# The SSD's products inside a chunk, each issued as two products on the two column halves of the array

## What is computed

```python
cs = jnp.cumsum(da, axis=-1)
causal = jnp.tril(jnp.ones((Q, Q), dtype=bool))
seg = cs[..., :, None] - cs[..., None, :]
lmat = jnp.where(causal, jnp.exp(jnp.where(causal, seg, 0.0)), 0.0)
cb = jnp.einsum('bclgn,bcsgn->bcgls', cm, bm)
y_diag = jnp.einsum('bcgls,bcgels,bcsgep->bclgep', cb, lmat, xdt)
...
y = y_diag + y_off + xs * d_skip.astype(f32).reshape(G, E, 1)
```

## Time and profile before

| | us |
|---|---|
| median of 3 runs | 2791.63 |
| lowest and highest run | 2790.51, 2798.21 |
| the profiled execution, its own time | 2796.33 |
| its span, first to last instruction | 2795.1 |
| TensorE busy in the span | 2762.6 (99%) |
| VectorE busy | 1732.2 (62%) |
| ScalarE busy | 1347.7 (48%) |

### The profile page before, as it was taken

The page is one execution under the profiler, slowest core; times in us unless marked ns, Lnnn a source line. Parts: engine busy times, 40 slices in busy tenths (PEclk is TensorE's granted clock), DMA queues, the critical chain, the costliest instruction groups (busy, mean ns, idle before and its releaser), DMA issues.

```text
span 2795.1 us, 40891 instructions
## 1 busy us (share of the span) xinstructions
PE 2762.6 (99%) x17151; PEld 2361.5 (84%) x17151; DVE 1732.2 (62%) x2043; ACT 1347.7 (48%) x1741; POOL 42.4 (2%) x71
## 2 busy tenths in 40 slices
PE   8999989999999999999999999999999999999998
PEld 7888887888888888888888888888888888888887
DVE  6787667654655655555555566556766656665675
ACT  6745434544554444434444545554554444443444
POOL 2000000000000000000000100000000000000001
PEclk9999999999999999999999999999999999999999
DMA  7565327566555656666666555555556555565553
GB/s 235 168 196 188 98 68 234 171 197 195 156 175 181 188 190 195 191 190 191 196 185 193 181 189 187 166 171 176 175 173 195 189 191 193 181 196 196 190 187 136
DMA packets 395317, 506.69 MB, mean 181 GB/s; under 512 B 11441, under 2 KB 287422, under 8 KB 394366
## 3 DMA queue, kind: packets, MB, share of 16 engines
q1 hardware_dynamic: 380925, 488.26, 54.3%
q10 hardware_dynamic: 14208, 15.81, 1.8%
HBM read 501.87 MB, written 2.17 MB: 180 GB/s over the span
## 4 chain that ended last, share of the span: by engine, by line
PE 96%; DVE 2%; ACT 1%; DMA 1%; issue 1%; ACTq 0%; SPq 0%; DVEq 0%
PE PS L697 38%; PE PS L702 34%; PE PS L706 17%; PE PS L952 3%; PE PS L745 1%; PE PS L1182 0%; PE PS L1162 0%; DVE wlo L2184 0%; PE PS L728 0%; PE PS L874 0%; PE PS L1239 0%; DMA slab<-in_x 0%; PE PS L890 0%; ACT whi L1495 0%; PE PS L855 0%
## 5 line engine op out<-in xcount | busy, mean ns | idle before, releaser
L2184 DVE TENSOR_TENSOR wlo<-raw,whi 128x1024 fp32r<-128x1024 f32 x922 | 1128.4, 1229 | 787.6 <-ACT whi L1495 783.6
L1495 ACT ACTIVATE whi<-raw 128x1024 fp32r<-128x1024 f32 x922 | 970.6, 1057 | 931.4 <-PE PS L706 454.8
L702 PE MATMUL PS<-XX,whi 128*128 128x512 f32 (+1 forms) x3856 | 1215.8, 396 | 0.2
L706 PEld LDWEIGHTS PS<-XX,wlo 128*128 128x128 f32 (+1 forms) x3856 | 724.4, 188 | 171.2
L706 PE MATMUL PS<-XX,wlo 128*128 128x256 f32 (+1 forms) x3856 | 759.6, 278 | 0.0
L697 PE MATMUL PS<-whi,act 128*128 128x512 f32 x2208 | 593.1, 390 | 0.0
L702 PEld LDWEIGHTS PS<-XX,whi 128*128 128x128 f32 (+1 forms) x3856 | 588.9, 189 | 3.1 <-issue 1.6
L697 PEld LDWEIGHTS PS<-whi,act 128*128 128x128 f32 x2208 | 411.8, 188 | 83.9
L697 PE MATMUL PS<-wlo,act 128*128 128x512 f32 x1104 | 339.9, 389 | 0.0
L697 PE MATMUL PS<-whi,XX 128*128 128x512 f32 x1024 | 280.7, 396 | 7.4 <-DVE wlo L2184 3.1
L697 PEld LDWEIGHTS PS<-wlo,act 128*128 128x128 f32 x1104 | 207.2, 188 | 43.4
(11 more groups left out here) (417 smaller groups left out, 1428.6 us busy)
## 6 DMA issues: line engine op xcount, KB each, us to landing
raw<-in_ffn_w SPq DMA_DIRECT2D x128, 1024.0 KB, 5.5
raw<-in_w_in SPq DMA_DIRECT2D x103, 1024.0 KB, 5.0
raw<-in_w_ffn_gate SPq DMA_DIRECT2D x44, 1024.0 KB, 4.9
raw<-in_w_ffn_up SPq DMA_DIRECT2D x44, 1024.0 KB, 4.9
raw<-in_w_ffn_down SPq DMA_DIRECT2D x44, 1024.0 KB, 5.2
raw<-in_w_out SPq DMA_DIRECT2D x32, 1024.0 KB, 5.2
raw<-in_xattn_wk SPq DMA_DIRECT2D x16, 1024.0 KB, 5.5
raw<-in_xattn_wv SPq DMA_DIRECT2D x16, 1024.0 KB, 5.0
```

Source lines behind the costliest of these rows:

```text
L702: T.matmul(ps[0:wd, f, :], whi[:, o:o + wd], b.x[:, kk, :], start=first, stop=False, skip_group_check=True)
L706: mm = T.matmul(ps[0:wd, f, 0:SEQ], wlo[:, o:o + wd], b.x[:, kk, 0:SEQ], start=False, stop=last, skip_group_check=True)
L1495: S.activation(k.whi[:, h % 4, 0:b.size], k.raw[:, t % 4, u * b.size:(u + 1) * b.size], ACT.Copy).then_inc(k.w_hi, 1)
L2184: V.tensor_tensor(k.wlo[:, h % 4, 0:b.size], k.raw[:, h // 2 % 4, u * b.size:(u + 1) * b.size], k.whi[:, h % 4, 0:b.size].bitcast(F32), AL ...
```

## The change

Each product of line 855 becomes two. The first takes tokens s 0 to 63 as rows and tokens l 0 to 63 as columns (64 rows by 64 columns, at the array's first row and first column) and writes partitions 0 to 63 of the bank. The second takes all 128 tokens s as rows and tokens l 64 to 127 as columns (128 rows by 64 columns, in the second column half), and writes partitions 64 to 127. The quarter of `Ldec` that is left out is zero by the mask. Both move the same 64 channels. Nothing else is changed; the semaphore's increment stays on the last product of a block.

```diff
         for e in range(4):
             h = 8 * g + 4 * q + e
-            mm = T.matmul(PS[:, ssd_bank(n), (4 * q + e) * 64:(4 * q + e) * 64 + 64], k.Ldec[n % 3][:, e, :],
-                          k.xdt[:, c, h * 64:h * 64 + 64], start=(q == 0 and e == 0), stop=True,
-                          skip_group_check=True)
+            L, out, own = k.Ldec[n % 3], slice((4 * q + e) * 64, (4 * q + e) * 64 + 64), slice(h * 64, h * 64 + 64)
+            T.matmul(PS[0:64, ssd_bank(n), out], L[0:64, e, 0:64], k.xdt[0:64, c, own], start=(q == 0 and e == 0),
+                     stop=True, skip_group_check=True)
+            mm = T.matmul(PS[64:P, ssd_bank(n), out], L[:, e, 64:P], k.xdt[:, c, own], start=(q == 0 and e == 0),
+                          stop=True, skip_group_check=True)
         mm.then_inc(sd.pe, 1)
```

## The result

| | us |
|---|---|
| before, median of 12 runs | 2790.78 (2789.32 to 2798.21) |
| after, median of 12 runs | 2796.57 (2796.03 to 2800.59) |
| ratio after/before | 1.0016, 95% interval 1.0009 to 1.0023 |
| the profiled execution after, its own time | 2796.29 |
| its span | 2795.1 |

The change makes the kernel slower by 0.16%: 4.5 us by the ratio (2.5 to 6.4), 5.8 us by the medians. It was forecast at +5.9 us, and as no change within 0.3%. How near to 5.9 the true difference lies, the interval leaves open.

What follows compares the result with a forecast made beforehand. TensorE, busy 99% of the span, was taken to bound the kernel. Holds add 8.2 us, less 1.1 hidden behind block 2 and 1.2 in instruction gaps: +5.9, so 2797.5 us; range 2788 to 2801.

Steps and rivals of the forecast that it cites:

- A change of rows alone holds TensorE: Inside line 855's blocks: each of seven inner changes between 64 and 128 rows costs a hold of 0.145 us.
- The side-by-side rival: In line 855's blocks: column halves run together without holds, a block takes 0.66 us, total 2789.2 us; chance 0.16.
- The price: Line 855's blocks: a half product takes 0.255 us, eight take 2.04 us instead of 1.04.
- The sum on TensorE: All eight blocks: 3.4 us for blocks 3, 4, 5, 7 plus 4.8 for the others, +8.2 us before cover.
- The term for block 2: Behind block 2 TensorE waits 0.94 us for line 2609, hiding all but 0.1 of the block's 1.2 us: -1.1.
- The instruction gaps: Between 352 and 361 us TensorE runs out of instructions, 2.5 us in all; slower blocks close half, -1.2 us.
- The three gaps I had looked at: TensorE's three idle times between 352 and 361 us, 2.5 us in all, expected to be about half after.
- 3.8 us for a batch: Time TensorE needs for 256 instructions of 64x64 work at 0.029 us a step; transfers come one per 4.2 us.
- The 4.6 at the lower end of the range: Whole kernel: 8.2 - 1.1 - 2.5, the added time if all 2.5 us of gaps hide it.
- what I called no change: Whole kernel: a difference within 0.3% (8.4 us), hardly measurable; chance of this outcome 0.82.
- the working with nothing covered: From 330 to 361 us: gaps stay and 128 more instructions add up to 1.9 us: 8.2 - 1.1 + 1.9 = +9.0.
- The slower rival: From 330 to 361 us: holds with nothing covering them, gaps stay, +9.0 to +10.1 us, 2801 us; chance 0.15.

Runs made afterwards that it cites:

- Experiment 1: The change with both half products on all 128 rows, so one shape; 2789.25 us against 2791.17 of before, ratio 0.9989 (0.9980 to 0.9998).
- the second trace: The kernel before, unchanged, profiled once more; stretch between two fixed VectorE instructions 119.3 us against 120.9 in the first trace, span 2788.4 us.
- experiment 4: The change in blocks 3, 4 and 5 alone, the other blocks as before; one trace, stretch 123.1 us against 120.9 of before.
- experiment 5: The change in block 2 alone, the other blocks as before; one trace, stretch 121.1 us against 120.9 of before.
- experiment 6: The kernel before with 64 more transposes (128 TensorE instructions) at the start of TensorE's program; stretch 120.2 us against 120.9, total 2796.0 us.
- experiment 3: The change with both products 64 rows by 64 columns, leaving out part of the computation; one trace, stretch 118.9 us against 120.9 of before.

## Why the prediction was right

- **A change of rows alone holds TensorE.** The step on which all rested, and the one that no row of before showed for 64 and 128 rows in the same columns. Experiment 1 takes the change of shape away, with as many instructions, and the block falls from 2.05 to 0.62 us. The side-by-side rival had the right speed for the two halves, and the wrong condition: they do run at once, 0.01 us apart, if their shapes agree.
- **The price.** 0.255 us for a half product, measured 0.256; a block 2.04, measured 2.05; after line 697 the first load 0.31 us behind the last matmul, measured 0.32. The drain that the Trainium skill names ("TensorEngine Tiling (Array Packing)", Tiling Modes) is this 0.15 us. It is the 64 elements' stream and, by an estimate, about 0.1 us behind it: the holds of 0.21 us after 256 elements and 0.31 after 512 leave 0.11 that does not grow with them.
- **The sum on TensorE.** 8.2 less 1.1 behind block 2 was 7.1; the rest column of the table gives 121.8 - 113.9 = 7.9 (8.1 against the second trace). The 8.2 was right: matched matmul by matmul, a block behind line 697 or 851 adds 1.21 or 1.22 us, and blocks 3, 4 and 5 alone (experiment 4) 0.86, 0.87 and 0.83. The term for block 2 was right in its mechanism (experiment 5 shows VectorE not later). It was 1.2 against the first trace of before and 0.7 against the second, whose wait for line 2609 is 0.49 us instead of 0.94. What the sum lacked is a wait that a gap had covered. The rows are of before, of the change and of experiment 6:

```profile
400.65 0.35 PE L952 MATMUL PS<-over_x,slab 64*64 64x64 f32 x9 [1.39 <-issue]
...
405.50 0.44 PE L867 MATMUL PS<-ident,slab 128*128 128x128 f32 x2 [1.01 <-DVE slab L2513]
...
406.05 0.44 PE L865 MATMUL PS<-ident,slab 128*128 128x128 f32 x2 [1.01 <-DVE slab L2513]
```

  In before a batch ends (number 9153) just ahead of the products of line 865. While TensorE waits for its instructions, VectorE ends what these need (line 2511 there, at 400.34 us), and TensorE finds it done. With the count moved by 128, in the change as in experiment 6, no such gap stands there, and TensorE waits 1.01 us for VectorE; 0.28 us of a later wait goes in return, and 0.8 stays. With it the sum is 8.2 - 1.2 + 0.8 = 7.8 against the first trace (measured 7.9) and 8.2 - 0.7 + 0.8 = 8.3 against the second (8.1). Experiment 6, which adds no work here, has a rest 1.2 us above before's; 0.8 of it is this wait.
- **The instruction gaps.** I took 1.2 us of cover. The table has 7.0 - 4.4 = 2.6 against the first trace of before and 1.2 against the second. The three gaps I had looked at closed but for 0.14 us (I had said half); others opened, 0.47, 1.25 and 0.28 us. That the gaps belong to the instructions' count is shown by experiment 6, and that slower work closes the next ones by experiment 4. Their size differs by 1.4 us between two executions of one kernel, so no sum can be closer here. One term was misread: 3.8 us for a batch came from loads that step by 0.029 us, but in the products behind 352.73 they step by 0.015, and the batch that begins there has all begun within 2.0 us, 1.75 us ahead of the next.
- **The total.** +5.9 forecast; +5.8 by the medians, +4.5 by the ratio (2.5 to 6.4). Against the first trace of before the last two points erred by 0.8 up and 1.4 down, against the second by 1.0 up and nothing; the stretch was longer by 5.3 and 6.9. So it is partly luck that the medians met the forecast so closely. The 4.6 at the lower end of the range is a sum; 8.4 is the bound of what I called no change, where the working with nothing covered gave 9.0.
- **The slower rival** needed the gaps to stay. They shrank.
- **What would beat it.** I had bounded a gain at 4.2 us and given the halves none. With equal shapes the kernel gains 1.9 us by the medians and 3.1 by the ratio (0.6 to 5.6; experiment 1). Its blocks are shorter by 2.6 us (0.22 us behind lines 697 and 851, 0.42 behind line 954, four each). In the stretch 2.1 of it is left against the first trace of before, whose gaps are as large, and 0.5 against the second, whose gaps are 1.3 us less; the wait of 1.01 us for VectorE is there too.

Not tried: three products of 64 rows by 64 columns for each head, which would need no hold at an edge towards line 954. Two of them would write the same partitions of one bank from different row halves; whether they may do so at the same time, or need a wait of their own, no run shows.

## What to carry to other kernels

Cutting work off a product pays only if the pieces keep one shape, or come in groups of one: here a half product with its change of shape took 0.256 us, more than the whole product of before (two loads at 0.111 us). If a product can be split into column halves, give both halves the same rows, zeros and all, and alternate them: here they ran at once. And read what follows the place before pricing it: a wait may cover it, and small instructions may have to be waited for in themselves.

## What the runs showed that I had not expected

TensorE's instructions come in batches of 256, and where its products are 64x64 it uses them up faster than they come (2.0 us for one batch at 352.73, the gaps' ends 3.7 and 4.4 us apart): 4.4 to 7.7 us of this stretch of 120 us are such waits, at numbers 256 apart in every trace. A kernel that makes its small products faster gets only part of it back (experiment 3: blocks 4.2 us shorter, the stretch 2.0 or 0.4), and the sizes vary by themselves by 1.4 us. Such a gap can also cover a wait for another engine, which shows when an added instruction moves the count. What asks for a batch, and when, is open. Also, one of the two traces of before waits 5 us longer between 439 and 464 us than the other, so a single profile's span is no measure of a change of this size.
